# Two gaps ahead of the matmul operand tiles: 832 and 384 bytes in place of one of 960

## What is computed

```python
D_MODEL = 2048; SEQ = 256; DEPTH = 2
# first block, layer i
u = rmsnorm(h) @ w_in[i]                       # 2048 x 5632
h = h + concatenate([ya, yb]) @ w_out[i]       # 2048 x 2048
h = h + rmsnorm(p[i] @ w_pe[i]) * sigmoid(h @ w_pg[i])
# second block, layer 0 and layer 1
p = rmsnorm(x) @ fox_w_in[0]; x = x + (fox_attention(p) * silu(gate)) @ fox_w_out[0]
p = rmsnorm(x) @ swa_w_in[0]; x = x + (swa_attention(p) * silu(gate)) @ swa_w_out[0]
```

## Time and profile before

| | us |
|---|---|
| median of 3 runs (1780.55 to 1784.65) | 1781.31 |
| the profiled execution | 1774.15 |
| its span, first to last instruction | 1772.4 |
| TensorE matmuls busy (14,349) | 1755.0 |
| TensorE weight loads busy | 1686.9 |
| VectorE busy | 1309.2 |
| ScalarE busy | 901.2 |

### The profile page before, as it was taken

How to read it: one execution, slowest core, us unless ns; L and a number is a source line. 1 busy time by engine, 2 the same in 40 slices (tenths; PEclk the granted TensorE clock), 3 DMA queues, 4 the chain that set the end, 5 groups by cost and what they waited for, 6 DMA issues and landing times.

```text
span 1772.4 us, 35680 instructions
## 1 busy us (share of the span) xinstructions
PE 1755.0 (99%) x14349; PEld 1686.9 (95%) x14349; DVE 1309.2 (74%) x2085; ACT 901.2 (51%) x1326; POOL 38.5 (2%) x48
## 2 busy tenths in 40 slices
PE   8999999999999999999999999999999999999997
PEld 8999999999999999999999899999989999999886
DVE  7899899977679987998777765656565556667754
ACT  5433665555533465456565463545455453665553
POOL 0000000000000000000000110100100000000000
PEclk9999999999999999999999999999999999999999
DMA  7666555555666664555566665665655556555563
GB/s 233 190 206 194 191 147 176 197 184 195 197 186 205 195 202 143 158 196 193 180 200 184 206 202 179 190 189 180 193 160 167 191 179 187 162 158 171 169 194 131
DMA packets 200082, 326.07 MB, mean 184 GB/s; under 512 B 14911, under 2 KB 66319, under 8 KB 199821
## 3 DMA queue, kind: packets, MB, share of 16 engines
q1 hardware_dynamic: 197085, 320.58, 57.9%
q10 hardware_dynamic: 2864, 3.62, 0.7%
HBM read 320.42 MB, written 2.69 MB: 182 GB/s over the span
## 4 chain that ended last, share of the span: by engine, by line
PE 92%; DVE 5%; DMA 1%; issue 1%; ACT 1%; ACTq 0%; DVEq 0%; POOLq 0%; SPq 0%; POOL 0%
PE g L499 73%; PE g L510 11%; DVE w_lo L898 2%; PE att L600 2%; PE att L645 2%; PE att L624 2%; DVE cacc L1144 2%; PE att L499 1%; ACT w_hi L1533 0%; DMA turned<-q 0%; PE att L789 0%; DMA stage<-in_w_in_dram 0%; DVE glu L1116 0%; PE att L858 0%; PE att L576 0%
## 5 line engine op out<-in xcount | busy, mean ns | idle before, releaser
L898 DVE TENSOR_TENSOR w_lo<-stage,w_hi 128x1024 fp32r<-128x1024 f32 x577 | 706.4, 1232 | 378.4 <-ACT w_hi L1533 377.4
L1533 ACT CAST w_hi<-stage 128x1024 fp32r<-128x1024 f32 x577 | 599.8, 1050 | 618.5 <-PE g L499 403.8
L499 PE MATMUL g<-a_hi,w_hi 128*128 128x256 f32 x2496 | 705.5, 283 | 1.6 <-DVE a_lo L1078 0.9
L499 PE MATMUL g<-a_lo,w_hi 128*128 128x256 f32 x2496 | 696.6, 279 | 0.0
L499 PE MATMUL g<-a_hi,w_lo 128*128 128x256 f32 x2496 | 696.5, 279 | 0.0
L499 PEld LDWEIGHTS g<-a_hi,w_hi 128*128 128x128 f32 x2496 | 469.9, 188 | 12.1 <-issue 8.4
L499 PEld LDWEIGHTS g<-a_lo,w_hi 128*128 128x128 f32 x2496 | 473.1, 190 | 0.0
L499 PEld LDWEIGHTS g<-a_hi,w_lo 128*128 128x128 f32 x2496 | 470.5, 189 | 0.5 <-issue 0.2
L499 PE MATMUL g<-b_hi,w_hi 128*128 128x256 f32 x1440 | 404.5, 281 | 0.1
L499 PE MATMUL g<-b_lo,w_hi 128*128 128x256 f32 x1440 | 401.5, 279 | 0.0
L499 PE MATMUL g<-b_hi,w_lo 128*128 128x256 f32 x1440 | 401.4, 279 | 0.0
(11 more groups left out here) (232 smaller groups left out, 1359.9 us busy)
## 6 DMA issues: line engine op xcount, KB each, us to landing
stage<-in_fox_w_in_dram SPq DMA_DIRECT2D x128, 512.0 KB, 3.7
stage<-in_w_in_dram SPq DMA_DIRECT2D x112, 512.0 KB, 3.8
stage<-in_swa_w_in_dram SPq DMA_DIRECT2D x72, 512.0 KB, 3.9
stage<-in_w_in_dram SPq DMA_DIRECT2D x128, 256.0 KB, 3.1
stage<-in_w_out_dram SPq DMA_DIRECT2D x64, 512.0 KB, 4.2
stage<-in_w_pg_dram SPq DMA_DIRECT2D x64, 512.0 KB, 4.1
stage<-in_fox_w_out_dram SPq DMA_DIRECT2D x32, 512.0 KB, 4.2
stage<-in_swa_w_out_dram SPq DMA_DIRECT2D x32, 512.0 KB, 4.0
```

Of the source, the lines that this page charges most:

```text
L499: mm = pe.matmul(acc[:, j * S:(j + 1) * S], w[:, slot, c0 + j * P:c0 + (j + 1) * P], xx[:, k, :], start=st and m == 0 and j % 2 == 0, stop ...
L898: dve.tensor_tensor(w_lo[:, slot, :], stage[:, slot, :], w_hi[:, slot, :].bitcast(F32), ALU.subtract).then_inc(*t.inc("w_split"))
L1533: act.copy(w_hi[:, slot, :], stage[:, slot, :]).then_inc(*t.inc("w_rounded"))
```

## The change

`apart` shrinks from 240 floats to 208 (832 bytes, 320 modulo 512). A second unused tile of 96 floats (384 bytes) is put between the pair `a` and the pair `b`, which so starts at 832 + 384 = 1216 bytes, 192 modulo 512. The two gaps together are 256 bytes longer than the one before. All that lies behind `b_lo` moves up by 256 bytes: `h` to `glu` from 448 to 192, `cacc` to `ones` from 384 to 128. `stage`, `w_hi` and `w_lo` stay. No instruction is added, removed or moved.

```diff
-APART = 240
+APART = 208
+BETWEEN = 96
...
         sb("apart", [APART])
         a_hi = sb("a_hi", [KT, S], F32R)
         a_lo = sb("a_lo", [KT, S], F32R)
+        sb("between", [BETWEEN])
         b_hi = sb("b_hi", [KT, S], F32R)
         b_lo = sb("b_lo", [KT, S], F32R)
```

## The result

The changed kernel takes 1781.99 us in the median of 12 runs, the kernel before 1777.64 in 12 runs beside it: a ratio of 1.0029, 95% interval 1.0017 to 1.0041. (The ratios are those on record; two medians divided give 1.0024 here, and can differ from a recorded ratio by some 0.1%.) It is slower, by some 4 to 5 us, where 20 us less had been forecast. The profiled execution is 1781.18 us with a span of 1779.4, 7.0 us above the profiled span of before.

A forecast was written before the change was run, and what follows sets the result against it. The prediction took TensorE's matmul pitch to bound the kernel. Line 499 was to gain 20 us and all other terms 0, so 1781.31 us became 1761, with a range from 1740 to 1808.

The forecast's parts named there:

- What bounds the kernel: TensorE's matmuls cover 1755.0 of 1772.4 us and hardly wait, so their pitch sets the end.
- The two rhythms: Line 499: the same matmul runs at 113.3 ns in some pieces and 117.8 in others.
- the stand-in for line 499: Line 789's mean of 114.3 ns taken for `a` and `b` at line 499, instead of 116.0: 20 us gained.
- the slow share: Line 499: 0.6 of 11,808 matmuls in the slow rhythm, from record lengths; 32 us of the span.
- `pe`: Small pair of 192 matmuls, 120.0 ns at 384, moving to 128: taken at 0, 1.3 us either way.
- Form N: Line 510, 756 matmuls with 512 streamed columns: taken at 0, bounds 10 us more and 7 us less.
- The baseline: 20 us taken off the 1781.31 us median, not off the profiled execution of 1774.15 us.
- The place does nothing: Rival: rhythms come from how a piece starts, so the time stays 1781 us; 15%.
- Farther is slower: Rival: at line 499, tiles farther from the multiple of 512 run slower, about 1802 us; 30%.
- Below 113.3: Rival: line 499 may go under 113.3 ns; all at 109 gives 1698 us, in part 1720 to 1748; 5%.
- What would show it: Signs if right: line 499's mean record falls from 279 towards 277 ns; long pieces at 118 run at 113 to 115.

The follow-up runs named there:

- the fastest heap: Kernel before, nothing changed: its executions lay in three groups near 1775, 1780 and 1785 us; this is the group near 1775.
- the run with `a` alone: Against the kernel before, only the pair `a` moved, from 448 to 320; `b` and all tiles behind stayed: 1781.98 us, ratio 1.0013.

## Why the prediction was wrong

- **What bounds the kernel** was read rightly: TensorE's pitch. The two rhythms and their prices of 113.3 and 117.8 ns held in every run at 448. Nothing else moved: the instruction that writes `q`, which went from 448 to 192, takes 1224 ns after and 1225 before.
- **The step that failed is the stand-in for line 499.** The forecast took line 789, because 320 and 192 occur in it, and noted that its loads of 32 columns make it a milder case. The runs show that it doesn't stand for line 499: at 0, where line 501 goes to 120.0 ns, it stays at 113.8, and with `a` at 480, where line 503 has 118.3, it goes to 116.9. In the changed kernel it passes through the same four places as before and stays at 114.4, while line 501 with `a` goes from 115.9 to 117.2. So its 114.3 ns said nothing of `a` at 320; that the length of the load makes the difference is likely but not shown, since line 789 also mixes places. The term was set at 20 us gained; it was 10.0 lost for `a` and 4.1 gained for `b`, as the slow share, worked out as (mean pitch less 113.3) / 4.4, went from 0.6 to 0.9 for `a` and to 0.35 for `b`. The row that did carry news of the place was `pe`: 120 ns at 384 stood against the best forecast there, and `a` and `b` at 384 went to 118.8.
- **`b` didn't move.** 448 to 192 is 256 bytes, one period. No row before could show the period; 4320 of the term's 11,808 matmuls were counted for a move that had no effect of its own. The gain of `b` came from `a`: the run with `a` alone has it whole.
- **Form N was taken at 0**; it costs 1.5 us with `a`, inside the bounds of 7 us less and 10 us more. **`pe`, taken at 0**, changed by 0.1 us.
- **The baseline.** The share of 0.6 slow was read from an execution of the fastest heap; in another execution of the same kernel the mean pitches are 116.5 and 116.9. The forecast was set against a median of 1781.31 from three runs, and twelve gave 1777.64.
- **The rivals.** "The place does nothing" fell at 0 and 384, with 1816 and 1809 us. It was right only for `b`, through the period; that its 1781 us lies beside the measured 1782 is luck, 10.0 lost and 4.1 gained set against a median of before that was 3.7 us too high. The forecast had drawn it from the Trainium skill's page "SBUF — State Buffer", section "Who interferes with whom", which calls TensorE's two read ports independent and states that it never waits on anyone. That no place could matter doesn't hold for this kernel; whether a port is what TensorE waits for isn't shown. "Farther is slower" had the right sign for `a` and the wrong law: 192 is farther than 320 and costs nothing, 480 is nearer than 448 and costs more. "Below 113.3" was seen nowhere at line 499: no place had a rhythm under 113.3, so no run here shows the 109.2 ns that the forecast worked out from the Trainium skill's page "TensorE: Matmul & The Clock Gate", section "Back-to-back issue gap". The page gives that formula for a matmul by itself, and says that in a stream of weight loads and matmuls both set the distance; the forecast left that out.
- **What would show it** held a bad test: the records' mean length. With `a` at 320 its pitch rose by 1.3 ns and the mean record stayed at 279 ns; a slow stretch there has records of 279 to 280 ns, not 281. The other test, the long pieces, was the one that spoke.

What stays open: why 448 is cheap, why a transpose leads into the fast rhythm there and into the slow one at 320, why the rhythm turns fast at the switch from `a` at 320 to `b`, and what the 4.4 ns are spent on. The runs show what it hangs on, not the mechanism under it.

## What to carry to other kernels

Where one shape of matmul runs at two pitches, divide long pieces of the chain by their counts before costing anything, and look at two executions, since one may be the best of several. The distance in SBUF between the loaded and the streamed operand is worth a scan in steps of 64 bytes over 256: it cost up to 2.2% here, and moving both operands together by 64 bytes showed no new price. A stand-in row must share every part that may cause the price, here the full weight load of 128 columns and one fixed place, not just the number that the change turns.

## What was not expected of the hardware

- The pitch of a matmul with 256 streamed float32r columns and a load of 128 depends on the distance between the two operands, with a period of 256 bytes: a mean of 115.6 to 116.9 ns at 448 or 192, 117.0 to 117.7 at 320 or 64, 118.8 at 384 or 128, 120.0 at 0. Behind these means stand 113.3 and 117.8 ns at 448, 192, 320 and 64, with other shares, 118.7 and 120.0 at 384 and 128, and 120.0 alone at 0. With 512 streamed columns it is another order: 227.3 at 0, 229.2 at 448, 232.4 at 384, 233.3 at 320.
- At one distance there are two pitches, 113.3 and 117.8 ns, which last over a thousand matmuls. How a piece is entered counts: a transpose ahead of three pieces with `a` gave 113.3 ns at 448 and 117.8 at 320. At two entries the rhythm differs between executions of one kernel: 9.9 us of 1774.
- One transpose of 109 ns ahead of a piece of 774 matmuls with `b` at 448 took 3.6 us off it (91.36 to 87.74).
